# Gate/up in pairs of column tiles: six of sixteen k tiles as 2x2 blocks, and hid turned by two wide transposes and sixteen SBUF copies

## What is computed

```python
def _swiglu(x, w_gate, w_up, w_down):
    return (jax.nn.silu(x @ w_gate) * (x @ w_up)) @ w_down
...
        x = _layer_norm(DEEPNORM_ALPHA * x + m, ln1_g, ln1_b)
        x = _layer_norm(DEEPNORM_ALPHA * x + _swiglu(x, w_gate, w_up, w_down), ln2_g, ln2_b)
```

## Time and profile before

| | |
|---|---|
| median of 3 runs | 931.61 us (931.35 to 931.75) |
| the profiled execution | 931.67 us |
| its span, first to last instruction | 929.9 us |
| PE / DVE / ACT / POOL busy | 923.4 / 773.7 / 513.4 / 95.9 us |
| granted TensorE clock | 1.000 |
| matmuls | 4406 |

### The profile page before, as it was taken

One profiled execution on the slowest core, in us unless ns is written; L12 is line 12 of the kernel. 1 busy time (PEld: TensorE's weight loads), 2 busy tenths in 40 slices (PEclk: granted clock), 3 DMA queues, 4 the chain that ended last, 5 costly groups with the idle time before them and its releaser, 6 DMA issues.

```text
span 929.9 us, 11643 instructions
## 1 busy us (share of the span) xinstructions
PE 923.4 (99%) x4406; PEld 774.5 (83%) x4406; DVE 773.7 (83%) x1049; ACT 513.4 (55%) x704; POOL 95.9 (10%) x84
## 2 busy tenths in 40 slices
PE   9999999999999999999999999999999999999997
PEld 8999988888878888888888888888888888888885
DVE  6778566578779898989999998988969997999777
ACT  5686765354464646555565646455545565456550
POOL 0205530000311020202011020000000000000000
PEclk9999999999999999999999999999999999999999
DMA  9744324584808375665648375756657656355632
GB/s 362 315 166 145 129 91 167 195 328 167 318 5 290 111 256 162 223 218 185 228 135 274 112 270 148 242 198 200 219 210 300 226 225 233 130 222 231 230 132 91
DMA packets 36759, 188.06 MB, mean 202 GB/s; under 512 B 4064, under 2 KB 4576, under 8 KB 22880
## 3 DMA queue, kind: packets, MB, share of 16 engines
q1 hardware_dynamic: 36672, 187.32, 56.4%
q0 software_dynamic: 32, 0.00, 0.0%
HBM read 183.11 MB, written 4.19 MB: 201 GB/s over the span
## 4 chain that ended last, share of the span: by engine, by line
PE 99%; DVE 0%; ACT 0%; DVEq 0%; issue 0%; ACTq 0%
PE acc L1983 26%; PE acc L2005 21%; PE acc L1758 9%; PE tp L1983 9%; PE acc L1966 6%; PE acc L1696 5%; PE tp L1966 4%; PE tp L2005 4%; PE acc L1617 4%; PE acc L1895 2%; PE tp L1935 2%; PE acc L1730 1%; PE tp L1809 1%; PE tp L1744 1%; PE tp L1822 1%; PE tp L1606 0%
## 5 line engine op out<-in xcount | busy, mean ns | idle before, releaser
L1983 PE MATMUL acc<-w_hi,act_t 128*128 128x512 f32 x720 | 227.3, 389 | 0.0
L972 ACT ACTIVATE w_hi<-raw 128x1024 fp32r<-128x1024 f32 x120 | 125.7, 1057 | 111.4 <-PE acc L1983 57.2
L1021 ACT ACTIVATE w_hi<-raw 128x512 fp32r<-128x512 f32 (+1 forms) x154 | 114.9, 782 | 100.3 <-PE acc L2005 88.0
L2005 PE MATMUL acc<-w_hi,hid_t 128*128 128x512 f32 x504 | 161.0, 389 | 0.0
L1424 DVE TENSOR_TENSOR w_lo<-raw,w_hi 128x512 fp32r<-128x512 f32 (+1 forms) x154 | 131.8, 881 | 33.2 <-ACT w_hi L1021 33.0
L1983 PEld LDWEIGHTS acc<-w_hi,act_t 128*128 128x128 f32 x720 | 135.1, 188 | 28.1
L1377 DVE TENSOR_TENSOR w_lo<-raw,w_hi 128x1024 fp32r<-128x1024 f32 x120 | 147.2, 1244 | 7.7 <-ACT w_hi L972 6.9
L1983 PE MATMUL acc<-w_lo,act_t 128*128 128x512 f32 x360 | 140.0, 389 | 0.0
L2005 PEld LDWEIGHTS acc<-w_hi,hid_t 128*128 128x128 f32 x504 | 94.6, 188 | 19.6
L2005 PE MATMUL acc<-w_lo,hid_t 128*128 128x512 f32 x252 | 98.0, 389 | 0.0
L1374 DVE TENSOR_TENSOR w_lo<-raw,w_hi 128x1024 fp32r<-128x1024 f32 x63 | 82.7, 1313 | 18.2 <-ACT w_hi L967 17.8
(11 more groups left out here) (262 smaller groups left out, 1582.2 us busy)
## 6 DMA issues: line engine op xcount, KB each, us to landing
raw<-in_w_pairs SPq DMA_DIRECT2D x120, 512.0 KB, 4.5
raw<-in_w_down SPq DMA_DIRECT2D x44, 1024.0 KB, 6.0
raw<-in_w_pairs SPq DMA_DIRECT2D x18, 1024.0 KB, 7.6
raw<-in_w_out SPq DMA_DIRECT2D x16, 1024.0 KB, 4.9
raw<-in_w_gu SPq DMA_DIRECT2D x8, 1024.0 KB, 10.7
raw<-in_x_w SPq DMA_DIRECT2D x14, 552.0 KB, 7.1
raw<-in_w_uq SPq DMA_DIRECT2D x4, 1024.0 KB, 6.1
raw<-in_w_ukv SPq DMA_DIRECT2D x4, 1024.0 KB, 4.8
```

The source lines that it names most:

```text
L972: act.activation(w_hi[:, v % RING, :], plain_raw(m), ACT.Copy).then_inc(hi_done, 1)
L1021: act.activation(unit_parts(u)[0], block_of(b, block, width), ACT.Copy).then_inc(down_hi_done, 1)
L1983: last = pe.matmul(out[:, t, :], act_t[:, k0 + m, x, t * P:(t + 1) * P], part[:, v % RING, m * GC:(m + 1) * GC], start=False, stop=(end an ...
L2005: last = pe.matmul(bank, lhs(x), part[:, cols * GC:(cols + 1) * GC], start=(first == u and (cols, x) == (0, 0) and part is hi_), stop=(end ...
```

## The change

`PAIR_K` goes from 4 to 6: three blocks by seven products, and ten k tiles (five plain steps a tile) remain. A product is now a "two" step (two blocks, 6 matmuls, 128x1024 weights) and a "third" step (one block, 3 matmuls, 128x512). The ring is eight places of 512 columns, and a step waits for whatever step last held its places. After each of P1, P5, P6 and P7 stands one plain step of the tile before (`second` 1 to 4, for pair 1 the last four halves of column tile 1). hid is turned by two transposes over all 128 partitions, each within its 32x32 blocks, into `local`, and SyncE then issues 16 copies from SBUF to SBUF of 32 partitions by 1 KB that put the blocks where they belong in `turned`.

```diff
-PAIR_K = 4
+BLOCKS = 3
+PAIR_K = 2 * BLOCKS
...
+        for product, end in zip((P1, P5, P6, P7), range(1, PLAIN)):
+            steps += [(p, "two", product), (p, "third", product), (p - 1, "second", end)]
+        steps += [(p, part, product) for product in (P2, P3) for part in ("two", "third")]
+        steps += [(p, "first", 0), (p, "two", P4), (p, "third", P4)]
+        steps += [(p, "first", n) for n in range(1, PLAIN)] + [(p, "second", 0)]
+    steps += [(PAIRS - 1, "second", n) for n in range(1, PLAIN)]
...
+HID_AT = 2
+BLOCK_MOVES = 16 * 16
...
-LAST_TURN = 11
+LAST_TURN = 5
+LAST_HID = 13
...
+    widths = [1 if kind == "third" else 2 for _, kind, _ in FFN_STEPS]
+    widths += [unit[3] for unit in DOWN_UNITS[:len(DOWN_UNITS) - LAST_LATE]]
+    at, places, before = 0, {}, {}
+    held = {x: V_PAIRS - RING + x // 2 for x in range(RING_BLOCKS)}
+    for v, width in enumerate(widths, V_PAIRS):
+        if at + width > RING_BLOCKS:
+            at = 0
+        places[v], before[v] = at, max(held[x] for x in range(at, at + width))
+        held.update((x, v) for x in range(at, at + width))
+        at = (at + width) % RING_BLOCKS
...
+            def move_blocks(p):
+
+                sp.wait_ge(local_done, p + 1)
+                for n in range(4):
+                    for b in range(4):
+                        sp.dma_start(turned[32 * b:32 * b + 32, n, :, :, :, :], local[32 * n:32 * n + 32, b, :, :, :, :])\
+                          .then_inc(ffn_turned, 16)
...
+                    if n == PLAIN_SLOTS and p < PAIRS - 1:
+                        load_quad(p + 1, 0)
+                        load_quad(p + 1, 1)
+                    if n == PLAIN_SLOTS + 1:
                         if p < PAIRS - 1:
-                            load_quad(p + 1, n - PLAIN)
-                        else:
-                            load_down(n - PLAIN)
+                            load_quad(p + 1, 2)
+                        move_blocks(p - 1)
             for b in range(2, RING):
                 load_down(b)
             sp.wait_ge(ffn_full, TILES)
             sp.wait_ge(x1_stored, 16)
             sp.dma_start(x1[:], x1_rows).then_inc(x1_back, 16)
+            move_blocks(PAIRS - 1)
             for b in range(RING, 2 * RING):
                 load_down(b)
...
                 act.wait_ge(ffn_full, i + 1)
+                if i == 1:
+                    act.wait_ge(g_lo, 1)
                 if i > 1:
-                    act.wait_ge(ffn_turned, i // 2)
+                    act.wait_ge(local_done, i // 2)
...
+                act.activation(s_gate[:, 0, :, :, :], g_sum[:, :, 0:2, :], ACT.Copy)
+                act.activation(s_third[:, 0, :, :], g_sum[:, :, 2, :], ACT.Copy).then_inc(g_hi, 1)
...
-                if (kind, n) == ("product", P5) and 2 <= p < len(DOWN_QUADS) + 2:
+                if (kind, n) == ("third", P5) and 2 <= p < len(DOWN_QUADS) + 2:
...
+            def turn_hid(p):
+
+                dve.wait_ge(ffn_hid, 2 * p + 2)
+                if p > 0:
+                    dve.wait_ge(ffn_turned, BLOCK_MOVES * p)
+                for i in range(2):
+                    dst = local[:, :, i, :, :, :].rearrange("p b c t s -> p t c b s")
+                    src = hid[:, i, :, :].rearrange("p t (c b s) -> p t c b s", c=2, b=4)
+                    last = dve.transpose(dst, src)
+                last.then_inc(local_done, 1)
...
+                if (kind, n) == ("third", P1):
+                    sum_1(p, "two")
+                    sum_1(p, "third")
+                if (kind, n) == ("second", 1) and p < PAIRS - 1:
+                    sum_3(p + 1, "two")
+                    sum_3(p + 1, "third")
+                if n == P5 and kind in ("two", "third"):
+                    sum_2(p, kind)
+                if n == P2 and kind in ("two", "third"):
+                    sum_4(p, kind)
+                if (kind, n) == ("first", 1):
                     add_y(p)
-                if kind == "first" and n >= 2:
-                    turn_hid(p - 1, n - 2)
+                    turn_hid(p - 1)
...
+                if u == LAST_TURN:
+                    turn_hid(PAIRS - 1)
...
+            for p in range(1, PAIRS):
+                if 0 <= p - 2 < len(DOWN_QUADS):
+                    factor_low(p - 2)
+                if p - 1 < len(DOWN_QUADS):
+                    factor_sums(p - 1)
```

373 lines of the change are left out of this document (196 added, 177 removed).

## The result

| kernel | median of the runs | profiled execution | its span | period of a pair (y_s) |
|---|---|---|---|---|
| before | 931.68 us (931.35 to 931.93) | 931.67 us | 929.9 us | 42.18 us |
| changed | 977.19 us (976.59 to 977.68) | 976.90 us | 975.1 us | 45.53 us |

The changed kernel is 4.9% slower: ratio 1.0488, interval 1.0470 to 1.0507. The forecast was 936.4 us in a range of 925 to 944. The direction was right and the size far off: 45.5 us in place of 4.8.

What follows compares the result with a forecast made beforehand. TensorE, busy 99%, was taken as the bound, VectorE second with 8% to spare. Matmuls -6.8, products +6.6, start +3.1 and last pair +1.9 gave +4.8 us: 936.4 us, range 925 to 944.

Steps and rivals of the forecast that it cites:

- What is taken away: TensorE in ten pairs: 30 matmuls fewer save 6.80 us, and a pair becomes 183 matmuls, 41.5 us.
- The copies: SyncE's queue in each pair: 16 issues of 0.33 us take 5.3 us, covered with 1.1 us in hand, cost 0.
- Rival C: Copies too late: over 0.4 us more each, or transposes of 3.5; one microsecond late gives 945, two 954; chance 0.09.
- Nobody wants the turned blocks before about 17: Readers of the copied blocks: none needs them until about 17 us after TensorE starts first 1, so cost 0.
- VectorE's average: VectorE's work per pair: 37.8 us of 41.5, with wide transposes of 0.87 us, so it keeps up by the average.
- The products: Pairs 2 to 10: TensorE waits for VectorE at second 2, 0.9 us plus 5.7 from GpSimd's exclusion, 6.6 us.
- the sign: TensorE's weight loads of second 2: idle 0.9 us with GpSimd's s_t beside VectorE's low part, 0.1 without.
- The start: Pair 1: waits of 1.05, 1.7 and 1.4 us, 4.15 in all, less the old 1.09; net +3.1 us.
- The last pair: Down projection's start: copies stand ahead of slots 4 and 5, so unit 10 waits; +1.9 us, bounds 0 to 5.
- Rivals A and B: A: covers hold, 925 to 928, chance 0.21. B: products stall half as often, about 931, chance 0.14.

Runs made afterwards that it cites:

- g4: e1 with sum_3 "two" moved behind second 2, sum_3 "third" behind P6's low parts, and ScalarE's s_t copy at first 4; 930.95 us.
- a1: The changed kernel with each pair's 16 copies issued behind the load of second 3, the last pair's left ahead of the down slots; 986.16 us.
- a2: a1 with the last pair's 16 copies also moved, behind the loads of down projection slots 4 and 5; 976.27 us.
- d1: The changed kernel with the 16 copies of a pair issued from GpSimd's queue, ahead of its sums, not from SyncE's; 993.66 us.
- b2: The kernel before, still two blocks, with wide transposes and 16 copies behind the loads, last pair's behind slots 4 and 5, s_t at first 0; 931.32 us.
- e1: a2 with the turned blocks' readers moved back: ScalarE's high part to second 3, its s_t copy to first 0; 937.32 us.

## Why the prediction was off, step by step

**What is taken away: right.** 4376 matmuls, and a pair without a wait takes 41.5 us by their pace. No version kept the gain: g4 is 0.6 us below the kernel before.

**The copies: the step that failed.** It read a copy's issue off the stores' 0.33 us. Measured: 0.59 us, one every 0.64, so 10.2 us in place of 5.3. The step had 1.1 us in hand and needed 4.9. Against `first` 1 the transposes end at +0.2 to +0.5 (forecast +0.9), and the load of `second` 1 is issued at +10.4 to +11.5 (forecast +6.2). In the pair shown ScalarE was free for it at +12.8 and had it at +15.3. The third quad load's issue of 1.5 us cost nothing: in every pair it ended before the transposes did. So the cost was not 0 but 4 us a pair.

Rival C was this case, but its own condition, over 0.4 us more per copy, was not met: 0.31 was enough, and by the 1.1 us in hand 0.07 would have been. The earlier trace rows had one store of 0.44 us, which the step for the last pair took as its bound; here it would have made 7.0 us in place of 5.3 and used up what was in hand. C's price, "one gives 945", counted the late load alone. The trace shows P5 and `second` 2 waiting again behind a late `second` 1, and the range ended at 944, below C's 945. C had a chance of 0.09, with "nothing in a row is as small as these copies" as its evidence. That was the row to take seriously: a size outside all rows, on a queue with one microsecond in hand, times nine. My estimate of 15 us for the 16, from the Trainium skill's table (DMA: Bandwidth & Descriptors, Bandwidth), missed the 10.2 by as much as the stores did, but on the right side of the limit; the table is for loads from HBM that GpSimd issues.

**"Nobody wants the turned blocks before about 17": wrong by a reader.** a1, a2 and d1 show that GpSimd's sums and behind them the `s_t` copy want them, and that ScalarE's whole queue stands behind that copy. In the changed kernel the copies came early enough to hide this.

**VectorE's average: right in its terms, less use than it seemed.** The wide transposes took 0.69 us (664 to 709 ns in 22), forecast 0.87. VectorE was busy for 36.0 us in the pair from 427.0 to 472.5, forecast 37.8. This was never the point; b2 shows that VectorE's relief by itself brings nothing.

**The products: the size came out by luck, in the kernel with its queue repaired.** e1 has a period of 42.44 us (line 1053, 282.9 to 664.9 over nine), forecast 42.4 for pairs 2 to 8. But the parts differ. The 0.82 us of exclusion is exact in the changed kernel, where it falls on `sum_3`; in e1 it does not stand among the products. The wait of 0.1 us at `second` 2 without `s_t` was 0.95 to 1.21 in five pairs of e1. In four of them VectorE begins `second` 1 2.9 to 3.6 us after TensorE has left `first` 4, not 2.00 as in the earlier trace rows, since the two `sum_1` are still ahead of it. I had taken VectorE as free at that moment. In the fifth (at 523.45 us) it begins at 2.00, and GpSimd's four sums hold it up instead. In the changed kernel `second` 2 waits 1.2 us in all nine pairs, the last two too, where the sign was 0.1.

**The start: right.** Waits of 4.7 us, forecast 4.15 (1.05, 1.7 and 1.4; measured 1.04, 2.03 and 0.46 with 1.21). The old wait of 1.09 went.

**The last pair: the mechanism right, the size over four times too small.** Forecast 1.9 us for one wait; measured 6.3 us of waits there and some 2.6 at half clock, and 5 more just ahead of it, where the copies of the pair before stand ahead of the last plain loads. That place the step didn't look at. The copies' 10.2 us for 5.3 stand ahead of the loads in both places. a2 takes away the waits in the down projection, and e1 the one of over 2 us ahead of it that a2 still has.

**Rivals A and B** needed the covers to hold. g4 has B's time with the covers repaired by hand, but not its parts: nothing waits at its end.

## What to carry to other kernels

Price a kind of transfer that no row shows by the dearest neighbour, and ask first who is queued behind it: on a queue with 1 us in hand a factor of two in the issue is paid in every iteration, and again by every step behind the late one. When something is moved later, move its readers too, and follow each reader to the queue that it stands in: copies late alone and readers late alone gave 1 us each, both together 40. Look at the clock too before you call a move worthless: the copies alone took 15 us of waits away and lost 11 us more at half clock. An engine's relief is worth nothing where it was not the one that ended a wait (b2), and in a full stretch without slack a late start costs again at each step behind it (here 1.4, 0.5 and 1.2 us in most pairs).
